# Two expert stages of a two-block model: spare weight chunks in unused stretches of the arena, and where the bias and norm rows are loaded

## What is computed

```python
def moe_ffn(h, router_w, router_b, w_gu, b_gu, w_down, b_down):      # first block
    logits = (hf @ router_w + router_b)
    top_logit, top_idx = lax.top_k(logits, TOP_K)                     # 4 of 32
    gates = jax.nn.softmax(top_logit, axis=-1)
...
    def expert_block(args):
        xb, e = args
        y = clamped_swiglu(xb @ w_gu[e] + b_gu[e])                    # 1024 x 2048
        return y @ w_down[e] + b_down[e]                              # 1024 x 1024
...
def hier_moe(v, w_grp, b_grp, w_exp, b_exp, w_gate, w_up, w_down):    # second block
...
    for e in range(MOE_N_EXPERTS):
        hdn = jax.nn.silu(vt @ w_gate[e]) * (vt @ w_up[e])            # 1024 x 512 each
        y = y + (combine[:, e:e + 1] * hdn) @ w_down[e]               # 512 x 1024
```

## Time and profile before

| | |
|---|---|
| median of 3 runs | 2130.63 us (2130.08 to 2131.89) |
| the profiled execution | 2130.74 us, span 2129.0 us |
| TensorE busy | 1953.1 us (92% of the span) |
| VectorE, ScalarE, GpSimd busy | 501.1, 322.6, 82.1 us |
| DMA | 707.15 MB, mean 332 GB/s |
| chain that ended last | DMA 15%, PE 5% of the span (it reaches back to the start of the second expert stage) |

### The profile page before, as it was taken

The page is one execution under the profiler, slowest core; times in us unless marked ns, Lnnn a source line. Parts: engine busy times, 40 slices in busy tenths (PEclk is TensorE's granted clock), DMA queues, the critical chain, the costliest instruction groups (busy, mean ns, idle before and its releaser), DMA issues. The chain is left out here.

```text
span 2129.0 us, 24746 instructions
## 1 busy us (share of the span) xinstructions
PE 1953.1 (92%) x10258; PEld 917.4 (43%) x10258; DVE 501.1 (24%) x1041; ACT 322.6 (15%) x576; POOL 82.1 (4%) x184
## 2 busy tenths in 40 slices
PE   6989999989999999999999999899899878778786
PEld 4677665643333333333333333345454422223232
DVE  2255544432122112221211211322342200000000
ACT  2134421210000000000000000213341100000001
POOL 2011031000000000000000000100020000000000
PEclk9999999999999999999999999999999899999999
DMA  9332167589999999999999999935254799999996
GB/s 338 121 129 80 49 243 260 225 341 427 428 428 428 428 428 428 428 428 428 428 428 428 428 428 428 362 119 171 62 202 172 286 428 428 428 428 428 428 428 274
DMA packets 98567, 707.15 MB, mean 332 GB/s; under 512 B 12315, under 2 KB 17933, under 8 KB 61517
## 3 DMA queue, kind: packets, MB, share of 16 engines
q1 hardware_dynamic: 98508, 706.36, 80.9%
HBM read 705.29 MB, written 1.05 MB: 332 GB/s over the span
## 5 line engine op out<-in xcount | busy, mean ns | idle before, releaser
L1707 PE MATMUL ps<-ring,arena 128*64 128x512 f32 x1536 | 337.5, 593 | 11.8 <-DMA ring<-in_moe_w_gu 11.8
L2932 PE MATMUL ps<-ring,arena 128*32 128x512 f32 x768 | 173.7, 616 | 42.5 <-DMA ring<-in_w_up 23.5
L1707 PEld LDWEIGHTS ps<-ring,arena 128*64 128x64 f32 x1536 | 109.8, 137 | 234.0 <-issue 206.5
L1734 PE MATMUL ps<-ring,arena 128*64 128x512 f32 x768 | 168.9, 592 | 0.0
L2155 PE MATMUL ps<-ring 128*128 128x512 f32 (+1 forms) x320 | 139.5, 586 | 0.7 <-ACT ring L2543 0.6
L1758 ACT ACTIVATE arena<-arena 128x512 f32<-128x512 f32 x32 | 20.1, 629 | 760.0 <-DVE arena L1789 760.0
L2932 PEld LDWEIGHTS ps<-ring,arena 128*32 128x32 f32 x768 | 52.6, 113 | 162.7 <-issue 160.4
L1707 PE MATMUL ps<-arena 128*64 128x512 f32 x512 | 113.5, 593 | 4.5 <-DMA arena<-in_moe_w_gu 4.5
L1079 PEld LDWEIGHTS ps<-arena 128*128 128x128 f32 x832 | 101.1, 200 | 35.3 <-issue 32.7
L1079 PE MATMUL ps<-arena 128*128 128x128 f32 x832 | 109.1, 289 | 2.3 <-DVE arena L1071 1.3
L1734 PEld LDWEIGHTS ps<-ring,arena 128*64 128x64 f32 x768 | 54.9, 137 | 109.9 <-issue 100.2
(11 more groups left out here) (601 smaller groups left out, 1989.0 us busy)
## 6 DMA issues: line engine op xcount, KB each, us to landing
ring<-in_moe_w_gu SPq DMA_DIRECT2D x96, 2048.0 KB, 28.4
ring<-in_moe_w_down SPq DMA_DIRECT2D x48, 2048.0 KB, 31.3
arena<-in_moe_w_gu SPq DMA_DIRECT2D x32, 2048.0 KB, 28.4
ring<-in_w_up SPq DMA_DIRECT2D x24, 2048.0 KB, 19.8
ring<-in_w_gate SPq DMA_DIRECT2D x24, 2048.0 KB, 26.9
ring<-in_w_down SPq DMA_DIRECT2D x24, 2048.0 KB, 27.0
ring<-in_w_in SPq DMA_DIRECT2D x22, 2048.0 KB, 8.2
arena<-in_moe_w_down SPq DMA_DIRECT2D x16, 2048.0 KB, 33.6
```

What stands on the lines that cost most here:

```text
L1707: last = M.matmul(ps[halves[j], 4 + which, :], xgT[buf][:, k, CAP * ee:CAP * ee + CAP], w[:, k2, at:at + 512], start=False, stop=(k == KD ...
L1734: last = M.matmul(ps[halves[j], 6, :], yT[:, k % KH, halves[k // KH]], w[:, k % KH, 512 * j:512 * j + 512], start=False, stop=(k == 2 * KH ...
L2932: last = M.matmul(ps[quads[e], 4 + which, :], xgT[:, k, quads[e]], w[e][:, k, :], start=(k == 0), stop=(k == KD - 1))
```

## The change

`ExpertLoads` takes a list `spare`: for each spare chunk the stretches of the arena that hold it in the first turn alone. The first stage gets one (2 x 2048 floats at 0 and 4096), the second two (2048 + 1024 + 1024 floats at 10752, 24576 and 22720, and 2 x 2048 floats at 0 and 4096). Chunks 8 (and 9) are then loaded in the stage ahead, and every later chunk sits `shift` slots earlier in the rotation. `load_first` issues a spare chunk as one DMA per stretch.

Since a stretch is not filled again, the rule for the first turn has two parts. Loads up to 15 + shift wait for chunk j - 8 - shift, later ones for chunk j - 8. `beside` issues the norm rows behind load 16 + shift, as their places hold the spare chunk until then. `bias_all` moves to arena 24064 and its loads go behind the second norm. `bsel1` moves into `masks`. TensorE's body becomes a function, called for the first turn ahead of the loop with `first_arrived`; the loop runs over the turns that are left.

```diff
+    def spare_slot(pieces, k, w):
+        rows = []
+        for at, n in pieces:
+            v = ar(at, n // w, w)
+            rows += [v[:, r, :] for r in range(n // w)]
+        return rows
...
         def load(self, sp, item, j):
             src, k, w = self.chunks(item + j // self.count)[j % self.count]
-            sp.dma_start(expert_slot(j % ESLOTS, k, w), src).then_inc(self.full[j % ESLOTS], 16)
+            n = (j - self.shift) % ESLOTS
+            sp.dma_start(expert_slot(n, k, w), src).then_inc(self.full[n], 16)
 
         def load_first(self, sp, slots):
             for n, freed, count in slots:
                 sp.wait_ge(freed, count)
-                self.load(sp, 0, n)
-
-        def load_rest(self, sp, items):
+                src, k, w = self.chunks(n // self.count)[n % self.count]
+                if n < ESLOTS:
+                    sp.dma_start(expert_slot(n, k, w), src).then_inc(self.full[n], 16)
+                else:
+                    row = 0
+                    for at, size in self.spare[n - ESLOTS]:
+                        sp.dma_start(ar(at, size // w, w), src[:, row:row + size // w, :]).then_inc(self.spare_full[n - ESLOTS], 16)
+                        row += size // w
+
+        def load_rest(self, sp, items, beside):
 
             n = sp.value_load(passes[0:1, 0:1], min_val=1, max_val=self.most)
             turns = items // self.unroll
 
-            for j in range(ESLOTS, self.turn):
-                sp.wait_ge(self.s_done, (j - ESLOTS) // self.per_done + 1)
+            for j in range(ESLOTS + self.shift, self.turn):
+                gone = j - ESLOTS if j >= 2 * ESLOTS + self.shift else j - ESLOTS - self.shift
+                sp.wait_ge(self.s_done, gone // self.per_done + 1)
                 self.load(sp, 0, j)
+                if j == 2 * ESLOTS + self.shift:
+                    beside(sp)
...
+        def first_arrived(self, pe, c, u, k=KD, w=512):
+            j = self.count * u + c
+            if ESLOTS <= j < ESLOTS + self.shift:
+                pieces = self.spare[j - ESLOTS]
+                pe.wait_ge(self.spare_full[j - ESLOTS], 16 * len(pieces))
+                return spare_slot(pieces, k, w)
+            n, arrivals = (j, 1) if j < ESLOTS else ((j - self.shift) % ESLOTS, (j - self.shift) // ESLOTS + 1)
+            pe.wait_ge(self.full[n], 16 * arrivals)
+            v = expert_slot(n, k, w)
+            return [v[:, r, :] for r in range(k)]
...
-    loads1 = ExpertLoads("experts1", gate_up_down, 6, 1, 4, MAXP)
-    bias_all, bias_dn = ar(5120, 512), ar(23040, 512)
-    bsel1 = (ar(5632, 4, CAP), ar(5888, 4, CAP))
+    loads1 = ExpertLoads("experts1", gate_up_down, 6, 1, 4, MAXP, [((0, 2048), (4096, 2048))])
+    bias_all, bias_dn = ar(24064, 512), ar(23040, 512)
+    bsel1 = [masks[:, 2 + 2 * i:4 + 2 * i, :].rearrange("p a b -> p (a b)").rearrange("p (s c) -> p s c", s=4) for i in range(2)]
...
-            sp.wait_ge(s_mT, 2)
+            loads1.load_first(sp, [(2, s_ada, 12), (3, s_mixg, 2), (4, s_mixg, 2), (5, s_mixg, 2), (0, s_wout, 7), (1, s_wout, 8)])
+            sp.wait_ge(s_h2, 2)
             for g in range(4):
                 sp.dma_start(bias_all[32 * g:32 * g + 32, :], b_gu[:, 512 * g:512 * g + 512]).then_inc(s_bgu, 16)
-            loads1.load_first(sp, [(2, s_ada, 12), (3, s_mixg, 2), (4, s_mixg, 2), (5, s_mixg, 2), (0, s_wout, 7), (1, s_wout, 8), (6, s_h2, 2), (7, s_lp, 2)])
+            loads1.load_first(sp, [(6, s_h2, 2), (7, s_lp, 2), (8, s_lp, 2)])
...
-                sp.dma_start(fg, row_everywhere(a["final_g"])).then_inc(s_p8, 16)
-                sp.dma_start(mg, row_everywhere(a["g_mix_2"][0])).then_inc(s_p8, 16)
+                def norm_weights(sp):
+                    sp.dma_start(fg, row_everywhere(a["final_g"])).then_inc(s_p8, 16)
+                    sp.dma_start(mg, row_everywhere(a["g_mix_2"][0])).then_inc(s_p8, 16)
...
-                n = loads.load_rest(sp, NE)
+                n = loads.load_rest(sp, NE, norm_weights)
...
-                with pe.Fori(0, n) as p:
-                    with pe.Fori(0, NE // UN) as q:
-                        for u in range(UN):
-                            i = p * NE + q * UN + u
...
+                for u in range(UN):
+                    expert(u, None)
+                with pe.Fori(1, n * (NE // UN)) as turn:
+                    for u in range(UN):
+                        expert(u, turn)
...
-    loads2 = ExpertLoads("experts2", gate_up_down2, 3 * QUAD, 2, 2, MAXP2)
+    loads2 = ExpertLoads("experts2", gate_up_down2, 3 * QUAD, 2, 2, MAXP2,
+                         [((10752, 2048), (24576, 1024), (22720, 1024)), ((0, 2048), (4096, 2048))])
...
-            loads2.load_first(sp, [(4, s_ls, NSUB), (5, s_ls, NSUB)] + rb2.last_uses() + [(6, s_n11, 2), (7, s_lp2, 2)])
+            ends = rb2.last_uses()
+            loads2.load_first(sp, [(4, s_ls, NSUB), (5, s_ls, NSUB)] + ends[0:2] + [(8, s_mxT, 2)] + ends[2:4]
+                              + [(6, s_n11, 2), (7, s_lp2, 2), (9, s_lp2, 2)])
...
-                sp.dma_start(gfin, row_everywhere(a["g_final_2"])).then_inc(s_p13, 16)
-                loads.load_rest(sp, NQ)
+                loads.load_rest(sp, NQ, lambda sp: sp.dma_start(gfin, row_everywhere(a["g_final_2"])).then_inc(s_p13, 16))
```

More of the change, by code:

```diff
@@ L996, in __init__ @@
             self.steps, self.rounds = self.turn // per_done, self.turn // ESLOTS
+            self.spare, self.shift = spare, len(spare)
             self.full = [sem(f"{name}_slot{n}_full") for n in range(ESLOTS)]
+            self.spare_full = [sem(f"{name}_spare{n}_full") for n in range(self.shift)]
             self.s_done = sem(f"{name}_slots_multiplied")
@@ new lines, in expert @@
+                def expert(u, turn):
+                    i = u if turn is None else turn * UN + u
+                    buf, ee = u // 2, u % 2
+                    pe.wait_ge(s_bs, i + 1)
+                    pe.wait_ge(s_GTt, i + 1)
+                    for which in range(2):
+                        for j in range(2):
+                            M.matmul(ps[halves[j], 4 + which, :], bsel[ee][:, 2 * which + j, :], bias_all,
+                                     start=True, stop=False)
+                    if ee == 0:
+                        pe.wait_ge(s_xgt, i + 2)
+                    for s in range(4):
+                        w = arrived(u, s, turn, 2, 2048)
+                        for k2 in range(2):
+                            k = 2 * s + k2
@@ L1694, in _ @@
                             for which in range(2):
                                 for j in range(2):
[L1696 to L1706, removed]
-                                            last = M.matmul(ps[halves[j], 4 + which, :], xgT[buf][:, k, CAP * ee:CAP * ee + CAP],
-                                                            w[:, k2, at:at + 512], start=False, stop=(k == KD - 1))
-                                last.then_inc(s_done, 1)
@@ L1727, in _ @@
[L1727 to L1738 removed]
+                                    at = 1024 * which + 512 * j
@@ new lines, in expert @@
+                                    last = M.matmul(ps[halves[j], 4 + which, :], xgT[buf][:, k, CAP * ee:CAP * ee + CAP],
+                                                    w[k2][:, at:at + 512], start=False, stop=(k == KD - 1))
+                        last.then_inc(s_done, 1)
+                    if ee == 0:
+                        pe.wait_ge(s_one, (0 if turn is None else turn * (UN // 2)) + buf + 2)
+                    pe.wait_ge(s_y2, i + 1)
+                    gather_half(x_tok, onehot, ee, 6, s_xg)
@@ new lines, in expert @@
+                    scatter()
+                    pe.wait_ge(s_y, i + 1)
+                    for k in range(KH):
+                        last = M.transpose(ps[:, 7, k * P:(k + 1) * P], y[:, k * P:(k + 1) * P], ident[:, :])
+                    last.then_inc(s_yT, 1)
+                    pe.wait_ge(s_gat, i + 1)
+                    for t in range(T):
+                        last = M.transpose(ps[:, 5, t * P:(t + 1) * P], gated[:, t, :], ident[:, :])
+                    last.then_inc(s_GT, 1)
@@ L2959, in _ @@
+                for u in range(2):
+                    quad(u, None)
+                with pe.Fori(1, n * (NQ // 2)) as turn:
+                    for u in range(2):
+                        quad(u, turn)
                 pe.wait_ge(s_GTt, n * NQ + 1)
```

137 lines of the change are left out of this document (64 added, 73 removed).

## The result

| | before | with the change |
|---|---|---|
| median | 2130.49 us of 4 runs (2130.08 to 2131.89) | 2116.8 us of 4 runs (2112.96 to 2118.41) |
| ratio, 95% interval | | 0.9939 (0.9916 to 0.9962) |
| the profiled execution | 2130.74 us, span 2129.0 us | 2115.71 us, span 2114.0 us |

A forecast was written before the change was run, and what follows sets the result against it. Both expert stages were taken to be bound by their weight streams at 428 GB/s. Gains of 1.5 us (first) and 8.6 us (second) made 10.1 us off 2130.74: 2120.6 us, range 2118.0 to 2123.2, including half a microsecond for run spread.

The forecast's parts named there:

- What bounds the kernel: Both expert stages: each ends a fixed time after its last weight byte, with DMA streams at 428 GB/s.
- Second stage, 8.6 us from 8.1 to 9.8: Second expert stage: two spare chunks save 9.8 us, the g_final_2 row costs 1.2, no hole; gain 8.6 us.
- The price for the split chunks: Spare chunks loaded in pieces: some 1.2 us more each at 341 GB/s, but they land in idle time.
- First stage, 1.5 us from 0 to 2.45: First expert stage: one spare chunk saves 4.9 us, a hole in the stream gives back 3.4; gain 1.5 us.
- The hole: First stream between loads 17 and 18: 3.4 us without weight loads; two rows fill 2.45, leaving 1.0 us empty.
- The rest I cost at nothing.: Moved biases, norm rows and selectors, and TensorE's first turn ahead of the loop: no effect on the time.
- rival C: TensorE's straight-line first turn stalls, lengthening the hole; gain under 4.3 us, about 2127 us; 0.07 together with E.
- The median of the runs is 0.1 us from that execution, so nothing is corrected.: Base of the forecast: the profiled execution's 2130.74 us is used as it stands, beside a median of 2130.63.
- A: First stage gives nothing or next to it, the hole being a chunk long; gain 8.1 to 9.0 us; 0.13.
- B: First stream has no hole, the queue's spread evens it out; gain 2.45 + 8.6 to 12.2 us; 0.13.
- D: Slower: rotated SBUF slots lower the streams' rate; 423 GB/s would give 2136.3 us; 0.05.
- E: Spare chunk lands behind chunk 9 of the stream; time within 0.2% of before; 0.07 together with rival C.

The follow-up runs named there:

- e_rows_late: The change with the first stage's two norm rows behind load 21 instead of load 17; ratio to before 0.9966.
- e_rows_end: The change with both stages' norm rows issued behind the last weight load of their stage; ratio to before 0.994.
- e_twice: The change with norm rows at the end and the first stage's spare stretch used twice, for chunks 8 and 17; 2110.7 us, ratio to before 0.9917.
- e_rest: The change without spare chunks and with the norm rows back at the start of both stages; ratio to before 1.0002.
- e_entry: The change with TensorE's first turn put inside two loops of one iteration each; ratio to before 0.9957.
- e_regs: The change with TensorE's first turn inside two loops and with waits on register values; ratio to before 0.9953.
- e_again: The change itself run and profiled once more, nothing altered; ratio to before 0.995.
- e_warm_after: The change plus 52 throwaway matmuls (fillers) in TensorE's waits; 2111.0 us, ratio to before 0.9925.
- e_best: The change with norm rows at the end, the first stage's spare stretch used twice, and throwaway matmuls in TensorE's waits; 2110.9 us, ratio to before 0.9912.
- e_warm_before: The kernel before plus the same throwaway matmuls in TensorE's waits; ratio to before 0.997.

## Why the prediction was right or wrong

- **What bounds the kernel.** Right. Both streams run at 428 GB/s in every profile, and all effects on the stages are bytes or holes of the streams.
- **Second stage, 8.6 us from 8.1 to 9.8.** Seven profiles with two spare chunks and the row at load 18 give 8.0 to 8.2, the lower end. The chunks are worth their 9.8 us; the row was mis-sized, 1.3 to 1.65 us by the base where bytes say 1.2. The isolated row had said 1.7, and I took the other end. The Trainium skill's rate for 1 MB ("DMA: Bandwidth & Descriptors", section "Bandwidth") gave an estimate of 1.5 us, which lies within what was measured. The price for the split chunks that I had worked out from the Trainium skill did not matter, as they landed in idle time.
- **First stage, 1.5 us from 0 to 2.45.** Six profiles with the spare chunk and the rows behind load 17 give 0.6 to 1.4, mean 1.1. The hole is shown, by e_rows_late, e_rows_end and e_twice; it costs 3.7 us, where I had 3.4. The rows were mis-sized here too (3.2 us for both against e_rest, 4.3 against before, not 2.45). They fill the hole and leave none of the 1.0 us of idleness. I had named the hole right and its fill wrong. It is luck that this moved the sum by 0.4 us only: 2.45 of rows and 1.0 of idleness, as I had it, come to nearly the same as the rows alone.
- **"The rest I cost at nothing."** This step failed in one term: the straight-line turn enters each stage 0.5 us sooner, 1 us in all, which I had only as a risk (rival C). The rule of the Trainium skill that straight code fares better than branches ("Runtime: NRT & Kernel Launch", section "Instruction fetch mechanics") points the right way, but e_entry and e_regs put more of it on waits on register values (0.25 and 0.16 us), which are no branch, than on the loops (0.17 and 0.08 us).
- **"The median of the runs is 0.1 us from that execution, so nothing is corrected."** This step failed most. Three runs within 1.8 us looked like a kernel with 2 us of scatter. It has 12, and the first runs and the profile were from its upper part, by chance as far as the record shows. In the profiles the differences outside the streams stand mostly where the clock is at half, and fillers shrink the scatter to 6.0 us; whether the clock makes the whole 12 us was not tried. Over 93 runs, before is at 2128.6 us. The terms as measured sum to 1.1 + 8.1 + 1.0 = 10.2 us. That this is within 0.1 of the forecast's sum is luck: two terms were too high by 0.9 together and one too low by 1.0. The change's 12 runs are 10.9 us lower than before's. So the 3.8 us between forecast and result are (rounded) 2.2 from a base that was too high, 0.1 from the sum of the terms, 0.7 that no term holds (the first pair's 1.7 us are a candidate), and 0.9 by which the first four runs of the change lie below its twelve.
- **Rivals.** A and B are out, C had the wrong sign, D and E are out. What I lacked was one in which the clock's falls move by some microseconds with any change of timing. Its half microsecond of range was far too little.

## What to carry to other kernels

In a stage that ends with its weight stream, a prefetched chunk is worth its whole transfer time, if the stream afterwards has no hole; count the loads still queued at the point where the extra buffer is used for the last time, and make that point late, when the stream has grown a backlog. Small loads that nobody needs before the end belong behind the last weight load, where they were free here, and not where a stretch happens to be empty. Before a few microseconds are read from a profile, take a second profile of the same kernel and line up the same instructions: whatever differs between the twins is the error of the reading.

## What the runs showed of the hardware that I had not expected

- A row of 4 KB spread over 128 partitions (0.52 MB) took 1.65 us in a full stream against before and 1.3 against e_rest; two in a row took 2.1 to 2.2 us each against before and 1.6 against e_rest. The same bytes of weights take 1.2 us.
- TensorE's clock was granted at half during the routers in every profile without fillers, and again behind the first experts, at 1369 us in e_again. In e_warm_after and e_best 52 matmuls of 128 columns in the waits removed these stretches in all three places; in e_warm_before one of 3.4 us was left at 1368 us. Between two executions of one kernel the stretch ahead of the first stage ended at different points of the work (6.70 and 5.23 us for the same gather).
- Two nested loops and waits on register values cost TensorE 0.4 us ahead of its first matmul in the first expert stage (1.33 to 1.75) and 0.24 us in the second (1.38 to 1.62).
- e_rest's first stage is 0.9 us longer than before's, without spare chunks and with the rows in their old place. No run tells why.
